# Mixture-of-experts layer on one core: the second stream of experts is ordered by matching two rankings instead of by a search step by step

## The reference, cut to what matters

```python
N_EXPERTS, TOP_K, D_EXPERT = 32, 4, 1024
top_val, top_exp = lax.top_k(h @ w_router + b_router, TOP_K)      # 512 tokens, 4 experts each
gate_w = jax.nn.softmax(top_val, axis=-1)
# for every expert e and every token x routed to it:
gt = jnp.minimum(x @ w_gate[e] + b_gate[e], 7.0)
up = jnp.clip(x @ w_up[e] + b_up[e], -7.0, 7.0)
y  = (gt * sigmoid(1.702 * gt) * (up + 1.0)) @ w_down[e] + b_down[e]
# output of a token: sum of its four y, weighted by gate_w
```

## Time and profile before

| | us |
|---|---|
| median of three runs | 1601.4 |
| the profiled execution | 1598.49 |
| its span in the profile | 1596.6 |
| TensorE busy | 1362.9 (85%) |
| VectorE busy | 813.7 (51%) |
| ScalarE busy | 198.0 (12%) |
| GpSimd busy | 279.8 (18%) |
| bytes moved by DMA | 488.17 MB, mean 306 GB/s |
| granted TensorE clock, mean | 0.903 of full |

### The profile page before, as it was taken

How to read it: one execution, slowest core, us unless ns; L and a number is a source line. 1 busy time by engine, 2 the same in 40 slices (tenths; PEclk the granted TensorE clock), 3 DMA queues, 4 the chain that set the end, 5 groups by cost and what they waited for, 6 DMA issues and landing times. The chain is left out here.

```text
span 1596.6 us, 39003 instructions
## 1 busy us (share of the span) xinstructions
PE 1362.9 (85%) x13038; PEld 564.4 (35%) x13044; DVE 813.7 (51%) x2993; ACT 198.0 (12%) x522; POOL 279.8 (18%) x214
## 2 busy tenths in 40 slices
PE   6999978989934985998899989896996999899852
PEld 3444444555511421332233333231342333233210
DVE  0229685555787543454356535353553455455424
ACT  0112245652000000000000000000000000000002
POOL 0001000014420210121122212121221122122100
PEclk8999989999956987998899989897997999899865
DMA  9831075745471799989998999979899899999994
GB/s 339 225 94 55 1 241 197 214 156 185 159 297 57 278 408 408 400 299 405 411 389 312 391 407 401 409 284 410 320 389 409 306 401 404 407 398 399 402 413 151
DMA packets 161699, 488.17 MB, mean 306 GB/s; under 512 B 40051, under 2 KB 59067, under 8 KB 144252
## 3 DMA queue, kind: packets, MB, share of 16 engines
q1 hardware_dynamic: 145532, 470.85, 76.1%
q0 software_dynamic: 16128, 16.82, 5.0%
HBM read 474.40 MB, written 17.77 MB: 308 GB/s over the span
## 5 line engine op out<-in xcount | busy, mean ns | idle before, releaser
L1074 PE MATMUL banks<-arena,misc 128*32 128x512 f32 x5248 | 654.0, 630 | 119.8 <-DMA arena<-in_w_up 94.0
L1074 PEld LDWEIGHTS banks<-arena,misc 128*32 128x32 f32 x5248 | 165.7, 113 | 502.3 <-issue 248.6
L1084 PE MATMUL banks<-arena,master 128*32 128x256 f32 x5248 | 331.5, 395 | 9.6 <-DMA arena<-in_w_down 6.4
L1900 DVE TENSOR_SCALAR cst<-banks 128x256 f32<-128x256 f32 x82 | 34.8, 425 | 402.8 <-PE banks L1074 401.2
L1084 PEld LDWEIGHTS banks<-arena,master 128*32 128x32 f32 x5248 | 168.5, 114 | 162.0 <-issue 72.5
L670 POOL DMA_INDIRECT misc<-moe_input,misc x84 | 88.3, 1052 | 673.9 <-DVE misc L1711 651.6
L686 POOL DMA_INDIRECT moe_output<-misc x82 | 130.2, 1587 | 236.2 <-issue 232.4
L1300 ACT ACTIVATE banks<-cst 128x256 f32<-128x256 f32 x82 | 31.8, 388 | 1001.8 <-DVE cst L1900 1001.8
L836 PE MATMUL banks<-arena 128*128 128x512 f32 x256 | 112.6, 595 | 0.0
L1682 DVE TENSOR_SCALAR master<-cbias 128x128 bf16<-128x128 f32 x340 | 94.8, 343 | 12.9 <-issue 8.0
L1476 DVE CUSTOM_DVE_ANT_0 arena<-banks,master 128x128 f32<-128x128 f32 (+3 forms) x96 | 46.0, 480 | 57.7 <-PE banks L936 54.3
(11 more groups left out here) (353 smaller groups left out, 1103.8 us busy)
## 6 DMA issues: line engine op xcount, KB each, us to landing
arena<-in_w_gate SPq DMA_DIRECT2D x256, 512.0 KB, 12.3
arena<-in_w_up SPq DMA_DIRECT2D x256, 512.0 KB, 14.0
arena<-in_w_down SPq DMA_DIRECT2D x128, 1024.0 KB, 16.1
arena<-in_w_ada SPq DMA_DIRECT2D x12, 2048.0 KB, 12.9
arena<-in_w_in SPq DMA_DIRECT2D x2, 2048.0 KB, 10.8
master<-bias_by_distance SPq DMA_DIRECT2D x16, 256.0 KB, 4.8
arena<-in_w_in SPq DMA_DIRECT2D x8, 256.0 KB, 4.3
arena<-in_cmp_k_w SPq DMA_DIRECT2D x2, 1024.0 KB, 6.3
```

The costliest lines, as they stand in the source:

```text
L1074: last = nc.tensor.matmul(two(bank[2 * b][strip(j), :]), hTe[:, k, :], arena[:, 24 * b + 2 * k:24 * b + 2 * k + 2, quarter(j)], start=Fals ...
L1084: last = nc.tensor.matmul(bank[2 * b + 1][strip(j), 0:256], actT[:, q, c, :], DN(b, q, c)[:, quarter(j)], start=False, stop=(q == 3 and c ...
```

## The change

The 22 rounds are gone. In their place the experts of B (FIRST_B, which is fixed, excepted) are ranked by size, the differences between neighbouring points of the curve ("wishes", the number of items wanted for each place) are ranked too, and the expert of size rank r goes to the place whose wish has rank r. Equal wishes are told apart by a small bit-reversed number (`mix`), which comes as 32 more columns of the constant `k_moe`, with one more load (4 KB) ahead of the weight loads. The curve is rounded to eighths (`ROUND`) so that equal wishes are equal. The last three lines write the place back.

```diff
-CHOSEN = NE - 10
-STEP, NONE_LEFT, OUT, LEFT = 256.0, 128.0, -6000.0, 8192.0
+ROUND = 1.5 * 2 ** 20
+FIRST_OF_B = 128 - (NE - 1)
...
             load("cst", tc, a["k_moe"][0:NE, M_TIE:M_W])
+            load("cst", mix, a["k_moe"][0:NE, M_MIX:M_MIX + NE])
...
-            pe.wait_ge(loaded("cst"), 48)
+            pe.wait_ge(loaded("cst"), 64)
...
-            dve.wait_ge(loaded("cst"), 48)
+            dve.wait_ge(loaded("cst"), 64)
...
-                link(nc.vector.tensor_scalar(passed, passed, 12288.0 - LEAD / RATE, -12288.0, ALU.add, ALU.add))
+                link(nc.vector.tensor_scalar(passed, passed, ROUND - LEAD / RATE, -ROUND, ALU.add, ALU.add))
                 row_of(passed, curve)
-                link(nc.vector.tensor_tensor(rises[:, 0:NE - 1], curve[:, 1:NE], curve[:, 0:NE - 1], ALU.subtract))
...
-                for k in range(CHOSEN):
-                    link(nc.vector.tensor_tensor_reduce(out=left_row, in0=gap_row, in1=gap_row, scale=-1.0, scalar=-NONE_LEFT * NONE_LEFT,
-                                                        op0=ALU.mult, op1=ALU.max, accum_out=nearest))
-                    link(nc.vector.tensor_scalar(chosen_row, left_row, nearest, None, ALU.is_equal))
-                    total_where(chosen_row, taken)
-                    link(nc.vector.scalar_tensor_tensor(gap_row, chosen_row, STEP * (k + 1), gap_row, ALU.mult, ALU.add))
-                    link(nc.vector.tensor_scalar(gap_row, gap_row, taken, rises[:, k:k + 1], ALU.add, ALU.subtract))
...
+                nc.vector.tensor_tensor(wish[:, 1:NE], curve[:, 1:NE], curve[:, 0:NE - 1], ALU.subtract)
+                nc.vector.tensor_scalar(candidate, tA, FIRST_OF_B + 0.5, 0.0, ALU.is_gt, ALU.add, accum_out=counted)
+                link(nc.vector.tensor_scalar(wish[:, 0:1], curve[:, 0:1], n_row[:, FIRST_B:FIRST_B + 1], None, ALU.subtract))
+                nc.vector.tensor_scalar(later, kth[:, 0:NE], counted, 512.0, ALU.is_ge, ALU.mult)
+                nc.vector.tensor_scalar(in_b, place, FIRST_OF_B + 0.5, None, ALU.is_gt)
+                link(nc.vector.tensor_tensor(wish, wish, mix, ALU.add))
+                link(nc.vector.tensor_tensor(wish, wish, later, ALU.add))
...
+                link(nc.vector.tensor_scalar(later, wish, own_wish, 0.0, ALU.is_lt, ALU.add, accum_out=wish_rank))
+                row_of(wish_rank, later)
...
+                link(nc.vector.tensor_scalar(same, later, size_rank, None, ALU.is_equal))
...
+                link(nc.vector.tensor_scalar(turn, turn, place, FIRST_OF_B + 1.0, ALU.subtract, ALU.add))
+                link(nc.vector.scalar_tensor_tensor(place, turn, in_b, place, ALU.mult, ALU.add))
+                row_of(place, tA)
```

More of the change, by code:

```diff
@@ L52 @@
 NOWHERE = 4096
+ROUND = 1.5 * 2 ** 20
 C_ID, C_TRI, C_IOTA, C_CMASK, C_CAUS, C_TV, C_W = 0, 128, 256, 384, 512, 640, 644
-M_J, M_IOTA, M_TIE, M_THR, M_K, M_PAR, M_E, M_W = 0, 1, 33, 66, 82, 210, 338, 339
+M_J, M_IOTA, M_TIE, M_THR, M_K, M_PAR, M_E, M_W, M_MIX = 0, 1, 33, 66, 82, 210, 338, 339, 339
 FIRST_A, FIRST_B = 0, 1
 RATE, LEAD, AFTER = 0.72, -0.5, 0.5
-CHOSEN = NE - 10
-STEP, NONE_LEFT, OUT, LEFT = 256.0, 128.0, -6000.0, 8192.0
+FIRST_OF_B = 128 - (NE - 1)
 def build_layer(nc, a, out):
@@ L213, in build_layer @@
         ccol = [ringf[0:NE, 23296 + n:23297 + n] for n in range(24)]
-        colt = ringf[0:NE, 23320:23321]
+        colt = [ringf[0:NE, 23320 + n:23321 + n] for n in range(4)]
         WP = ringf[0:NE, 23328:23408].bitcast(bf16)
@@ L218, in build_layer @@
         Wf = ringf[0:NE, 23440:23568]
-        gap_row, left_row, dup_row, chosen_row = (ringf[0:NE, 22592 + 64 * n:22624 + 64 * n] for n in range(4))
-        curve, rises = (ringf[0:NE, 22848 + 64 * n:22880 + 64 * n] for n in range(2))
+        wish, candidate, later, same = (ringf[0:NE, 22592 + 64 * n:22624 + 64 * n] for n in range(4))
+        mix = ringf[0:NE, 24224:24224 + NE]
+        curve = ringf[0:NE, 22848:22880]
         trib = identb
@@ L1784, in _ @@
             (rank, cum, total, inA1, sumA, gap, fill, inA, turn, second, place, nA, before, rest, start, pos, nB, pairs, ending,
-             shift, kcol, ends_at, passed, nearest) = ccol[0:24]
-            taken = colt
+             shift, kcol, ends_at, passed, counted) = ccol[0:24]
+            in_b, own_wish, wish_rank, size_rank = colt
             n_row, key_row, key_col, n_col = n33[:, 0:NE], key[:, 0:NE], key[:, NE:NE + 1], n33[:, NE:NE + 1]
@@ L1804, in switching_curve @@
                 link(nc.vector.tensor_scalar(passed, passed, kcol, 1.0 / RATE, ALU.add, ALU.mult))
-                link(nc.vector.tensor_scalar(passed, passed, 12288.0 - LEAD / RATE, -12288.0, ALU.add, ALU.add))
+                link(nc.vector.tensor_scalar(passed, passed, ROUND - LEAD / RATE, -ROUND, ALU.add, ALU.add))
                 row_of(passed, curve)
-                link(nc.vector.tensor_tensor(rises[:, 0:NE - 1], curve[:, 1:NE], curve[:, 0:NE - 1], ALU.subtract))
             def order_second_stream():
-                nc.vector.tensor_scalar(dup_row, tA, 128.0 - (NE - 1) + 0.5, OUT, ALU.is_le, ALU.mult)
@@ L1812, in order_second_stream @@
-                link(nc.vector.scalar_tensor_tensor(gap_row, tie[:, 0:NE], 1.0 / 1024, n_row, ALU.mult, ALU.add))
-                link(nc.vector.tensor_tensor(gap_row, gap_row, dup_row, ALU.add))
-                link(nc.vector.tensor_scalar(gap_row, gap_row, n_row[:, FIRST_B:FIRST_B + 1], curve[:, 0:1], ALU.add, ALU.subtract))
-                for k in range(CHOSEN):
-                    link(nc.vector.tensor_tensor_reduce(out=left_row, in0=gap_row, in1=gap_row, scale=-1.0, scalar=-NONE_LEFT * NONE_LEFT,
-                                                        op0=ALU.mult, op1=ALU.max, accum_out=nearest))
-                    link(nc.vector.tensor_scalar(chosen_row, left_row, nearest, None, ALU.is_equal))
-                    total_where(chosen_row, taken)
-                    link(nc.vector.scalar_tensor_tensor(gap_row, chosen_row, STEP * (k + 1), gap_row, ALU.mult, ALU.add))
-                    link(nc.vector.tensor_scalar(gap_row, gap_row, taken, rises[:, k:k + 1], ALU.add, ALU.subtract))
@@ new lines, in order_second_stream @@
+                link(nc.vector.tensor_tensor(wish, wish, later, ALU.add))
+                link(nc.vector.tensor_tensor_reduce(out=tC, in0=wish, in1=ident[0:NE, 0:NE], scale=1.0, scalar=0.0,
+                                                    op0=ALU.mult, op1=ALU.add, accum_out=own_wish))
+                nc.vector.tensor_scalar(same, tA, place, None, ALU.is_lt)
+                link(nc.vector.tensor_scalar(later, wish, own_wish, 0.0, ALU.is_lt, ALU.add, accum_out=wish_rank))
+                row_of(wish_rank, later)
@@ new lines, in order_second_stream @@
+                link(nc.vector.tensor_tensor_reduce(out=tC, in0=same, in1=candidate, scale=1.0, scalar=0.0,
+                                                    op0=ALU.mult, op1=ALU.add, accum_out=size_rank))
+                link(nc.vector.tensor_scalar(same, later, size_rank, None, ALU.is_equal))
+                link(nc.vector.tensor_tensor_reduce(out=tC, in0=same, in1=kth[:, 0:NE], scale=1.0, scalar=0.0,
+                                                    op0=ALU.mult, op1=ALU.add, accum_out=turn))
@@ L1967, in constants @@
     cst[:, C_TV:C_TV + QT] = np.arange(QT)[None, :] * P + p
-    moe = np.zeros((P, M_W), np.float32)
+    moe = np.zeros((P, M_MIX + NE), np.float32)
     moe[:, M_J] = 4 * NOWHERE + np.arange(P) // GT
@@ L1978, in constants @@
     moe[:, M_E] = np.arange(P) - NE
+    moe[:, M_MIX:M_MIX + NE] = [int(f"{k:05b}"[::-1], 2) / 256 for k in range(NE)]
     return {"k_cst": cst, "k_onehot": onehot, "k_moe": moe}
```

## The result

| | before | after |
|---|---|---|
| median, us | 1601.9 (4 runs, 1599.23 to 1602.48) | 1588.3 (4 runs, 1586.65 to 1591.35) |
| ratio after / before | | 0.9921 (95%: 0.9901 to 0.9940) |
| the profiled execution, its span | 1598.49, 1596.6 | 1586.65, 1584.8 |

The change is faster by 0.8%, 12.6 us by the ratio. Measured again in a later series, the changed kernel stood at 0.9938 (0.9924 to 0.9952) of the kernel before. The forecast was -7.4 us, 1594.0, with a range from 1587 to 1605.

The account below looks back on a forecast made before the run. VectorE's ordering was taken to bound the kernel before the tables, late loads or late buffers at expert switches after; -26.0 (tables) + 0 + 18.6 (order) = -7.4 us, from 1601.4 to 1594.0, range 1587 to 1605.

Parts of the forecast that it names:

- The bound before the tables: From about 469 us VectorE alone is the bound, so a shorter ordering moves everything behind it forward.
- The size of the stretch: VectorE's ordering, 29.55 us with 22 rounds, would take 3.5 us: gain 26.0 us (24.1 to 26.7).
- The clock at the restart: Item 0's last chunks and item 1's first matmuls stay near half clock: 0 taken, at most 3 us more saved.
- The small load: One more small load ahead of the weights costs SyncE at most 1.19 us, hidden by idle DMA time: 0 taken.
- The order's places: Load queue idle 7.95 us ahead of loads 7, 12, 16, 19, 23 and 18.6 ahead of load 25.
- The order's size: Load queue's idle time grows from 39.8 to 58.4 us under the new order: 18.6 us lost (16 to 20).
- The sum: Whole kernel: -26.0 + 0 + 18.6 = -7.4 us, from 1601.4 to 1594.0 us.
- The order costs nothing: Rival: the load queue makes up for idle time or load 25 is released earlier; 1575.4 us, chance 0.10.
- the tables give back less: Rival: loads in flight take over or saved instructions count only busy time; 4 to 10 us stay, 1598 to 1604, chance 0.08.
- The order isn't the one I listed: Rival: a slip in the new ordering arithmetic gives another order; between 1575 and 1615 us, chance 0.03.
- Ranks don't correct themselves: Rival: ranking errors add up, each late B switch costs 10.65 us; one 1604.7 (chance 0.06), two 1615.3 (two or more 0.07).

Follow-up runs that it names:

- Experiment 1: Changed kernel with the experts' places copied from a constant holding the old order, so old order with short tables; 1572.1 us, 0.9825 of the kernel before.
- experiment 6: Changed kernel with 60 more linked VectorE instructions behind the ordering, so the tables come later; 1602.2 us, 1.0026 of the kernel before.
- new order, long tables: Kernel before with its 22 rounds kept and their result overwritten by a constant holding the new order; 1614.4 us, 1.0093 of the kernel before.
- Experiment 4: Changed kernel with equal wishes told apart in rising instead of bit-reversed order, one constant changed; 1668.8 us, 1.0442 of the kernel before.
- experiment 5: Changed kernel with another permutation as the mix constant, chosen out of 300 by the recurrence; 1571.9 us, 0.9828 of the kernel before.

## Why the prediction was right, point by point

- **The bound before the tables: right.** VectorE alone held everything behind it. Experiment 1 carries 27 us to the end of the kernel, and experiment 6 takes 12 of them back one for one, within 2 us. One reading ahead of it was too strong: of the 119.8 us before the costliest group the row gives 94.0 to weight loads, which is not nearly all. Nothing in the sum rests on it.
- **The size of the stretch: right.** 3.38 us against 3.5; 26.2 us less than before instead of 26.0. The measured distances between linked instructions decided. The Trainium skill ("VectorE: DVE Perf Modes", section on the TRN2 errata) has a formula for the duration, by which the estimate was 19.7 us, 6.5 too little; the durations themselves, 0.18 us against 0.19 by the formula, agree.
- **The clock at the restart: inside its bounds, and luck.** I took 0, with up to 3 us possible. In the profiled pair 1.45 us came on top, which is a part of the difference between -7.4 and -11.8. But it isn't the change's: item 1's first 48 matmuls took 5.36 us in "new order, long tables" after a pause of 30.65 us, and 6.66 in "old order, short tables" after one of 4.98. The changed kernel and experiments 4 and 5 differ only in the values of one constant and have 5.36, 5.36 and 6.70.
- **The small load: right.** Its issue took 0.5 us of SyncE's time (1.68 us for two loads of `k_moe` instead of 1.19 for one), and the weight loads behind it were issued at 430.63 instead of 429.85. The tables did not wait for it.
- **The order's places: right.** The idle times ahead of loads 7, 12, 16, 19, 23 and the long one ahead of load 25 are all there. The distances up to load 14 are unchanged: in the profiled pair its bias load is issued 410.2 us behind that of load 2, and 410.4 before.
- **The order's size: the term that was mis-sized.** 18.6 us in the sum, 16.6 measured between items 1 and 81, and the bounds of 16 and 20 held it. The packets show where the 2 us are: in the gaps themselves, which grew by 16.6. The long one lasted 17.8 us instead of 18.6, and the short ones 6.9 to 7.6 instead of 7.95 each; the sum had five of them on both sides and let them cancel, but those of the kernel before took 36.5 us together and those of the changed one 35.2 (36.0 in its other trace, where the long one lasted 18.2). What the text named as a way to be below 18.6, loads that gathers no longer slow, was not it here: outside the gaps the 30 loads took 993.9 us before and 993.2 after.
- **The sum.** -27.2 + 16.6 - 1.1 = -11.7 in the profiled pair, -7.4 forecast. The difference is 1.2 us at the start of the items, where the clock's 1.45 is more than all of it, 2.0 from the order and 1.1 from the last stage, for which the sum had no term. All three fell the same way, so nothing cancelled. The medians of the first series lie 13.6 apart, the ratios give 12.6 and 9.9. The forecast of -7.4 lay in neither interval (the second one's ends at -7.7), so it was somewhat too small, by 2 to 5 us. The median of 1588.3 also lies below the 1590 to 1599 that the bounds of the parts gave and only 1.3 us inside the range of 1587 to 1605: the mechanism was right, and the range held by a small margin.
- **The rivals.** "The order costs nothing" fell by experiments 1 and 2, "the tables give back less" by 1 and 6. "The order isn't the one I listed" fell, since every gap is at its listed place. "Ranks don't correct themselves" asked for switches later than listed, and none came. What its heading names was already in the forecast as the 18.6 us: one B item too many by load 23, not made good before load 25. Experiment 4 shows how dear it gets when the ties fall badly (some 80 us from one constant).

## What to carry to other kernels

When two streams share one load queue and each waits for its own buffer, look at each switch for whether the load or the buffer is late, and write the four-number recurrence (pace, release to start, end of load to end of item, load time): it placed every idle time of five orders here, each within about 1 us of its length, and a good order can be looked for in it before anything is built, as experiment 5 did. A serial stretch of small dependent instructions on the one engine that everything waits for costs its whole length; count it by measured distances, not durations. And a cheaper way to make a decision has to be judged by the decision too: here 26 us of faster ordering bought a worse order that cost 16, and another constant kept both.

## What the runs showed of the hardware that was not expected

- Item 1's first 48 matmuls took 5.36 us, all at full clock, or 6.66 to 6.96, with about the first 3 us at half clock, without regard to how long TensorE had paused before the tables: 5.36 after 30.65 us and after 5.45, 6.81 after 31.60, 6.66 after 4.98, 6.96 after 15.88. A difference of 1.5 us between two single traces at such a place need not be an effect of an edit.
- With TensorE kept busy through the pause (1.26 us were left of 5.45) the group before ran at full clock and the next one had the half-clock stretch: 1.7 us won, 1.6 lost, in one execution.
